# Stick-breaking attention: value products put directly ahead of a step's scores

## What is computed

```python
q, k, v, gate = jnp.split(h @ w_in, 4, axis=-1)
q = rms_norm(q.reshape(Bn, T, SB_HEADS, SB_DH), q_norm_g)
k = rms_norm(k.reshape(Bn, T, SB_HEADS, SB_DH), k_norm_g)
...
z = jnp.einsum('bqhd,bshd->bhqs', q_blk, k, preferred_element_type=f32) * scale
mask = key_pos[None, :] < q_pos[:, None]
log1m = jnp.where(mask, -jax.nn.softplus(z), 0.0)
after = lax.cumsum(log1m, axis=3, reverse=True) - log1m
wts = jnp.where(mask, jnp.exp(jax.nn.log_sigmoid(z) + after), 0.0)
return jnp.einsum('bhqs,bshd->bqhd', wts.astype(v.dtype), v)
...
return (o * jax.nn.silu(gate)) @ w_out
```

## Time and profile before

| | |
|---|---|
| median of 3 runs | 1789.55 us (1789.54 to 1789.56) |
| the profiled execution, its own time | 1792.42 us |
| its span, first to last instruction | 1790.6 us |
| mean granted TensorE clock | 0.997 of full speed |
| TensorE (matmul) busy | 1745.0 us, 97% |
| VectorE / ScalarE / GpSimd busy | 890.1 / 824.1 / 664.6 us |
| the loop over pairs, first scores to last value products | 585.9 to 778.05 us |

### The profile page before, as it was taken

The page is one execution under the profiler, slowest core; times in us unless marked ns, Lnnn a source line. Parts: engine busy times, 40 slices in busy tenths (PEclk is TensorE's granted clock), DMA queues, the critical chain, the costliest instruction groups (busy, mean ns, idle before and its releaser), DMA issues.

```text
span 1790.6 us, 22578 instructions
## 1 busy us (share of the span) xinstructions
PE 1745.0 (97%) x8776; PEld 1421.5 (79%) x8776; DVE 890.1 (50%) x1326; ACT 824.1 (46%) x1191; POOL 664.6 (37%) x241
## 2 busy tenths in 40 slices
PE   7999999999999999999999999999999999999999
PEld 5688789888898666678788888888877877888887
DVE  6765954353233677744744334341187477435510
ACT  5575343685233667744422222222366724338720
POOL 1333420244435555444344444444323334104443
PEclk9999999999999999999999999999999999999999
DMA  4223210222222111112222222222222132012222
GB/s 173 94 71 95 71 42 7 95 93 85 105 95 72 47 48 48 40 58 102 83 95 100 105 99 94 94 94 94 83 95 94 56 110 63 10 48 95 94 95 71
DMA packets 48776, 143.70 MB, mean 80 GB/s; under 512 B 28080, under 2 KB 30256, under 8 KB 32816
## 3 DMA queue, kind: packets, MB, share of 16 engines
q1 hardware_dynamic: 48688, 142.50, 23.3%
HBM read 137.25 MB, written 5.24 MB: 80 GB/s over the span
## 4 chain that ended last, share of the span: by engine, by line
PE 73%; issue 17%; POOL 4%; ACT 3%; DVE 3%; DMA 0%; POOLq 0%; SPq 0%; DVEq 0%; ACTq 0%
PE ps L1633 19%; PE ps L1635 18%; PE ps L1634 18%; POOL w_lo L456 4%; PE ps L1896 2%; PE ps L1952 2%; PE ps L1923 1%; PE ps L2077 1%; PE ps L1938 1%; PE ps L1947 1%; PE ps L2123 1%; PE ps L1907 1%; PE ps L2021 1%; PE ps L2023 1%; PE ps L2022 1%
## 5 line engine op out<-in xcount | busy, mean ns | idle before, releaser
L456 POOL TENSOR_TENSOR w_lo<-w_raw,w_hi 128x2048 fp32r<-128x2048 f32 x107 | 505.3, 4723 | 805.7 <-ACT w_hi L587 802.5
L1633 PE MATMUL ps<-h_hi,w_hi 128*128 128x512 f32 x1488 | 597.9, 402 | 24.7 <-DVE w_lo L1019 9.9
L1635 PE MATMUL ps<-h_hi,w_lo 128*128 128x512 f32 x1488 | 583.0, 392 | 0.0
L1634 PE MATMUL ps<-h_lo,w_hi 128*128 128x512 f32 x1488 | 582.5, 391 | 0.0
L1633 PEld LDWEIGHTS ps<-h_hi,w_hi 128*128 128x128 f32 x1488 | 281.0, 189 | 103.4 <-issue 25.7
L1635 PEld LDWEIGHTS ps<-h_hi,w_lo 128*128 128x128 f32 x1488 | 280.9, 189 | 60.1
L1634 PEld LDWEIGHTS ps<-h_lo,w_hi 128*128 128x128 f32 x1488 | 281.4, 189 | 56.0 <-issue 1.4
L587 ACT ACTIVATE w_hi<-w_raw 128x2048 fp32r<-128x2048 f32 (+1 forms) x126 | 238.7, 1894 | 129.6 <-PE ps L1635 123.8
L1634 PE MATMUL ps<-y_lo,w_hi 128*128 128x512 f32 x448 | 174.5, 389 | 0.0
L1635 PE MATMUL ps<-y_hi,w_lo 128*128 128x512 f32 x448 | 174.5, 389 | 0.0
L1633 PE MATMUL ps<-y_hi,w_hi 128*128 128x512 f32 x448 | 174.5, 389 | 0.0
(11 more groups left out here) (209 smaller groups left out, 2343.9 us busy)
## 6 DMA issues: line engine op xcount, KB each, us to landing
w_raw<-w_tiles SPq DMA_DIRECT2D x124, 1024.0 KB, 4.9
x<-x_t SPq DMA_DIRECT2D x4, 512.0 KB, 6.7
out_t<-x SPq DMA_DIRECT2D x8, 256.0 KB, 5.6
w_raw<-w_tiles SPq DMA_DIRECT2D x2, 512.0 KB, 5.0
scr_u<-lt SPq DMA_DIRECT2D x8, 128.0 KB, 2.7
u_blk<-scr_u SPq DMA_DIRECT2D x2, 512.0 KB, 3.3
scr_v<-v_blk SPq DMA_DIRECT2D x2, 512.0 KB, 2.6
scr_t<-v_t SPq DMA_DIRECT2D x2, 512.0 KB, 3.6
```

Source lines behind the costliest of these rows:

```text
L456: pool.tensor_tensor(w_lo[:, slot, :], w_raw[:, slot, :], w_hi[:, slot, :].bitcast(F32), ALU.subtract).then_inc(lo_done, 1)
L1633: pe.matmul(out_, w_h, m_h, start=start, stop=False)
L1634: pe.matmul(out_, w_h, m_l, start=False, stop=False)
L1635: return pe.matmul(out_, w_l, m_h, start=False, stop=stop)
```

## The change

In the body of a step, the value products of step g-2 go from behind the scores, the sums of squares and the first projection blocks to the front, directly ahead of the scores. The projection blocks that stood on either side of them now follow each other. Nothing else is touched.

```diff
                 for v in range(4):
                     g = 4 * j + v
+                    if g >= 2:
+                        pv(g - 2)
                     z(g)
                     if more and v == 3:
                         sums(j + 1, 1)
                     fill(2 if more else 1)
                     if more and v == 1:
                         sums(j + 1, 0)
-                    if g >= 2:
-                        pv(g - 2)
                     fill(1 if more else 0)
                     if g:
                         cum(g - 1)
```

## The result

The changed kernel is a little slower: median 1793.38 us (1790.72 to 1795.42, 17 runs) against 1789.55 us of the kernel before (17 runs beside it). The ratio is 1.0018, 95% interval [1.0011, 1.0024]; on 1789.55 us that is +3.2 us, with +2.0 to +4.3. The profiled execution took 1795.35 us of its own, 2.9 more than the one before. The forecast was +3.0 us, most likely within 0.2%.

What follows compares the result with a forecast made beforehand. TensorE, 97% busy, bounds the kernel, but later scores lengthen the path through ScalarE. First pair 1.0, middle pairs 1.6, last 0.4 sum to +3.0 us on 1789.55, about 1792.5; range 1789.5 to 1795.2.

Steps and rivals of the forecast that it cites:

- The saving on switches: TensorE, head-pair loop: fewer switches between value products and other matmuls save 0.20 us a step, 6.0 in 30 steps.
- The prediction's other count: Switches on TensorE counted as tiling mode changes: one of four saved, 0.1 us in 30 steps, 3.0 us in all.
- The passage from value products to scores: TensorE, value products directly ahead of scores: taken at 0.09 us, already within the value products' own time.
- the hidden weight load: Rival, 12%: scores' weights load under the value products, three passages a pair each 0.1 us shorter; +0.8 us, 1790.3.
- the dearer switch: Rival, 18%: going from value products to scores costs 0.1 us more in three passages a pair; +5.2 us, 1794.7.
- The path from z1: Middle pair, from step 1's scores through ScalarE's softplus and weights to the next pair's first scores: 0.25 us later.
- z2: Scores of step 2 in a pair (z0 to z3 by step): 4.99 us behind step 1's scores, still early enough.
- w1: Step 1's weights, exponentials ScalarE writes to sb_w (w0 to w3 by step): back to back, 0.65 us long.
- pv1: Step 1's value products, 256 wide, 0.58 us (pv0 to pv3: 0.37, 0.58, 0.80, 1.01): start 0.05 behind their weights.
- the rival of slower copies: Rival, 3%: VectorE gets slower where its copies meet others on GpSimd, some 1 us a pair; about 1799 us.
- The pairs: Head-pair loop, 586 to 778 us: first pair +1.0 us, six middle pairs +0.26 each, last pair +0.4.
- TensorE alone counts: Rival, 4%: ScalarE's path has 1.2 us of slack a pair, so the whole 6.0 us saving shows; 1783.5 us.

Runs made afterwards that it cites:

- the kernel with short logarithms: Changed kernel with the softplus logarithm of steps 2 and 3 cut to one column per head, so its weights are not the layer's: 1783.49 us, ratio 0.996.
- the kernel before with the same logarithms: Kernel before the change, with the logarithms of steps 2 and 3 cut to one column per head: 1789.29 us, ratio 0.9992.
- steps 0 and 2 alone: Against the kernel before, value products moved ahead of the scores in steps 0 and 2 only: 1786.59 us, ratio 0.9978.
- the same swap: Kernel before with only ScalarE's square of step 2 moved behind that step's softplus: 1791.2 us, ratio 1.0006.

## Why the prediction was right

- **The saving on switches**, forecast as 0.20 a step, 0.80 a pair and 6.0 over the loop: 0.86 a pair, from the two kernels with short logarithms, and 5.9 us less of TensorE's busy time in the loop. The prediction's other count, by which three changes of shape out of four stay and the gain is 3.0, does not fit either figure.
- **The passage from value products to scores**, taken as contained in their own time: so it was, at all four widths. That rules out both rivals on it, the hidden weight load (0.1 shorter) and the dearer switch (0.1 longer).
- **The path from z1.** Forecast against the trace, in us behind z1 (638.29): z2 4.99 and 4.96; w1 9.63 and 9.62; pv1 10.33 and 10.32; z3 10.91 and 10.90; softplus of step 3 12.26 and 12.23; end of w2 17.31 and 17.30; next z0 18.16 and 18.15. From z0 to z1 it was 6.15 and 6.16. w1 went back to back and 0.65 long, as said.
- **The copy on VectorE** stood 5.97 us behind z1, forecast 5.99, and the scaling ahead of it took 1.21 us: the rival of slower copies fell.
- **The pairs**: middle +0.26 forecast, +0.24 on the mean; first +1.0 and +0.97; last +0.4 and +0.16. The last was the one term without a path worked out, and it was too large by 0.24. The loop lost 2.55 us where 3.0 was forecast. Behind it nothing was absorbed, as assumed: from the last value products to the start of TensorE's last matmul it was 1009.04 us before and 1009.06 after.
- **How near the total came is in part luck.** The runs say +3.2, but their medians carry the spread by the granted clock (last section). The loop's 2.55 is the better measure of the change, and against it the forecast is 0.45 too high.
- **TensorE alone counts** (1783.5) was wrong for the change, but it is what the middle pairs of the kernel with short logarithms do: their path through ScalarE has the slack that this rival asked for. That the median of that kernel is 1783.49 us is chance. Its loop is 4.27 us shorter than that of the kernel before with the same logarithms, not 6.0; TensorE is still idle in it for 2.44 us (185.60 less 183.16 busy), against 0.69.
- What the prediction did not see, though the row was there: the path need not have run through VectorE's copy at all. I took the square ahead of the softplus as given. And it valued the change as a whole; step by step, the same rows would have shown that pv0 and pv2 cost nothing (steps 0 and 2 alone have no wait in a middle pair) and pv1 its whole length.

## What to carry to other kernels

A saving on the busiest engine is worth something only if the move that brings it does not lengthen a chain through the others that binds, or comes to bind by it: measure both from the same starting point, for each place where the move is made, and keep it only in the places where there is slack. An engine 99.6% busy may still have a second chain of almost the same length beside it. When an engine waits for one thing while what it needs next has landed, swap the two in its order, but only once the chain binds: in the order before, the same swap was worth nothing in a middle pair.

## What the runs showed of the hardware

I had not expected that the runs of one kernel would be spread by the granted clock more than the change moved them. The 17 runs of the changed kernel go with it: from 1790.72 to 1791.55 us at a mean clock of 1.000, 1795.35 and 1795.42 at 0.997. In the rounds of the experiments the kernel before had eleven runs at a mean clock of 1.000, from 1788.33 to 1788.91 us. At that clock the two kernels' medians (1790.84 and 1788.45) are 2.4 us apart, near the 2.55 of the loop. Two stretches behind the loop, in the kernel before:

```profile
870.00:890.00 20.00, 17.83 (x72) 14.36 (x72) 17.59 (x22) 9.53 (x11) 4.61 (x1) 0.92 0.30 106
890.00:910.00 20.00, 20.00 (x89) 16.52 (x89) 7.95 (x6) 3.75 (x5) 9.20 (x2) 1.00 0.27 91
```

in the changed kernel:

```profile
870.00:890.00 20.00, 17.82 (x79) 14.50 (x78) 19.24 (x22) 7.23 (x9) 4.61 (x1) 1.00 0.25 88
890.00:910.00 20.00, 20.00 (x83) 16.32 (x82) 9.16 (x8) 6.43 (x7) 9.20 (x2) 0.91 0.19 70
```

and with value products ahead in steps 0 and 2:

```profile
870.00:890.00 20.00, 17.82 (x79) 14.45 (x78) 17.61 (x18) 8.51 (x9) 7.93 (x2) 1.00 0.16 57
890.00:910.00 20.00, 20.00 (x90) 16.57 (x89) 8.70 (x9) 5.43 (x5) 8.80 (x3) 1.00 0.30 106
```

All three had TensorE idle for 2.2 us in the first stretch, 870 to 890 us. Then in one the granted clock was 0.92 in that stretch, in one 0.91 in the next, and in the third it stayed at 1.00; from the last value products to the start of TensorE's last matmul the first two took 1009.04 and 1009.06 us, the third 1007.46. So such a dip cost 1.6 us here. What decides whether and when it comes, with the same idle time ahead of it, was not settled by these runs. This spread is why the pairs of the loop, at a clock of 1.00 in all kernels, say more on this change than the runs' medians, and why the 3.8 us between the two medians should not be set against the loop's 2.55.
